# Depthwise convolution of the latent steps as products with diagonal matrices, with bias and SiLU at the bank's reading

## The reference, cut to what matters

```python
def depthwise_conv_centred(u, w, b):          # u (1, N, 768), w (768, 5), b (768,)
    ch, width = w.shape
    rhs = jnp.transpose(w)[:, None, :].astype(u.dtype)
    out = lax.conv_general_dilated(u, rhs, window_strides=(1,), padding=[(width // 2, width // 2)],
                                   dimension_numbers=("NWC", "WIO", "NWC"), feature_group_count=ch)
    return out + b

xbc = jax.nn.silu(depthwise_conv_centred(xbc, lp["ssd_conv_w"], lp["ssd_conv_b"]))
```

## Time and profile before

| what | value |
|---|---|
| median of 3 runs | 2536.7 us (2534.78 to 2538.18) |
| the profiled execution's own time | 2540.28 us |
| its span, first to last instruction | 2538.4 us |
| PE busy | 1435.2 us (57%) |
| DVE busy | 1544.1 us (61%) |
| ACT busy | 272.6 us (11%) |
| POOL busy | 1460.7 us (58%) |
| DMA | 969.43 MB, mean 382 GB/s |
| mean granted PE clock | 0.715 of full |

### The profile page before, as it was taken

One profiled execution on the slowest core, in us unless ns is written; L12 is line 12 of the kernel. 1 busy time (PEld: TensorE's weight loads), 2 busy tenths in 40 slices (PEclk: granted clock), 3 DMA queues, 4 the chain that ended last, 5 costly groups with the idle time before them and its releaser, 6 DMA issues.

```text
span 2538.4 us, 20653 instructions
## 1 busy us (share of the span) xinstructions
PE 1435.2 (57%) x6676; PEld 610.3 (24%) x6676; DVE 1544.1 (61%) x4131; ACT 272.6 (11%) x667; POOL 1460.7 (58%) x1540
## 2 busy tenths in 40 slices
PE   6899757897332544365557786888510333332365
PEld 2455522372011211013212253356000000000000
DVE  0348975687887456556472687487799545457501
ACT  1321131111000010010000122211000000000000
POOL 0003527546657567766666646554747777777772
PEclk9889877997666656667767787799655555665666
DMA  9987999999979999999999999998969999999997
GB/s 371 403 336 294 395 380 382 370 404 374 378 288 411 413 410 410 410 411 412 412 411 377 379 412 342 373 351 337 395 253 406 409 409 409 409 409 410 410 409 301
DMA packets 238045, 969.43 MB, mean 382 GB/s; under 512 B 26314, under 2 KB 28746, under 8 KB 227954
## 3 DMA queue, kind: packets, MB, share of 16 engines
q0 software_dynamic: 221184, 805.40, 80.6%
q1 hardware_dynamic: 16754, 162.71, 15.6%
HBM read 964.87 MB, written 3.15 MB: 381 GB/s over the span
## 4 chain that ended last, share of the span: by engine, by line
DMA 37%; PE 22%; DVE 18%; POOL 14%; issue 7%; ACT 2%; SPq 0%; DVEq 0%; ACTq 0%; POOLq 0%
DMA ring<-peer_v_in,vidx 17%; POOL ring L645 8%; DMA work<-peer_v_in,vidx 7%; DMA work<-peer_u_in,idx 7%; DVE ring L1798 6%; PE psum L978 6%; POOL work L645 5%; DMA ring<-peer_u_in,idx 4%; PE acc L1024 4%; PE psum L954 3%; DVE work L1798 2%; PE psum L735 2%; POOL wring L645 2%; PE psum L690 1%; PE acc L662 1%
## 5 line engine op out<-in xcount | busy, mean ns | idle before, releaser
L645 POOL DMA_INDIRECT ring<-peer_u_in,idx x492 | 465.0, 945 | 523.5 <-DVE idx L1491 207.8
L1798 DVE CUSTOM_DVE_ANT_0 ring<-ring,h_kept 128x1024 f32<-128x1024 f32 x492 | 581.8, 1218 | 256.8 <-DMA ring<-peer_u_in,idx 249.4
L645 POOL DMA_INDIRECT ring<-peer_v_in,vidx x478 | 459.7, 962 | 252.8 <-issue 119.4
L1024 PE MATMUL acc<-ring,vw 128*32 128x512 f32 x1752 | 341.0, 852 | 365.7 <-DMA ring<-peer_v_in,vidx 340.0
L1798 DVE CUSTOM_DVE_ANT_0 work<-work,h_kept 128x1024 f32<-128x1024 f32 x208 | 249.8, 1220 | 178.7 <-DMA work<-peer_u_in,idx 173.0
L1024 PE MATMUL acc<-work,vw 128*32 128x512 f32 x672 | 150.3, 931 | 324.7 <-DMA work<-peer_v_in,vidx 306.3
L645 POOL DMA_INDIRECT work<-peer_v_in,vidx x226 | 215.0, 951 | 100.9 <-issue 57.2
L645 POOL DMA_INDIRECT work<-peer_u_in,idx x208 | 196.7, 946 | 117.8 <-issue 54.0
L1024 PEld LDWEIGHTS acc<-ring,vw 128*32 128x32 f32 x1752 | 49.9, 128 | 609.4 <-issue 595.4
L735 PE MATMUL psum<-wring,work 128*128 128x512 f32 (+1 forms) x432 | 176.2, 566 | 18.7 <-ACT work L1097 11.5
L978 PE MATMUL psum<-work,wring 128*128 128x256 f32 (+1 forms) x896 | 167.4, 352 | 2.9 <-ACT work L1066 2.9
(11 more groups left out here) (226 smaller groups left out, 1696.0 us busy)
## 6 DMA issues: line engine op xcount, KB each, us to landing
wring<-w_in_in SPq DMA_DIRECT2D x17, 2048.0 KB, 10.4
wring<-peer_wq_in SPq DMA_DIRECT2D x14, 2048.0 KB, 10.4
wring<-mod_w_in SPq DMA_DIRECT2D x10, 2048.0 KB, 13.1
ring<-mod_w_in SPq DMA_DIRECT2D x9, 2048.0 KB, 10.7
wring<-w_out_in SPq DMA_DIRECT2D x8, 2048.0 KB, 10.6
work<-mod_w_in SPq DMA_DIRECT2D x5, 2048.0 KB, 14.2
ring<-peer_u_in,idx POOLq DMA_INDIRECT x492, 11.9
ring<-peer_v_in,vidx POOLq DMA_INDIRECT x478, 8.5
```

Of the source, the lines that this page charges most:

```text
L645: nc.gpsimd.indirect_dma_start(slots[slot_of[n]], None, table, bass.IndirectOffsetOnAxis(ap=at[:, col + r:col + r + 1], axis=0))\
L1024: ins = mm(acc[half][lane:lane + QUAD, :], w[:, at:at + QUAD], two[j - pair][0][:, half * CHUNK:(half + 1) * CHUNK], start=(r == 0), stop= ...
L1798: V.tensor_tensor_reduce(held, held, h_kept[:, :], 1.0, 0.0, ALU.mult, ALU.add, dots[:, dots_at(k, t) + r:dots_at(k, t) + r + 1]).then_inc ...
```

## The change

In the latent steps (`st.lat`) the middle taps on ACT and the 24 tap additions on DVE go. For each block ACT makes five 128x128 diagonal matrices, each the identity scaled by the per-partition tap weight; two sets of five are held in `L.diag`, in the space of the rotary scratch, so the first two wait for the rotary embedding to be done, and each later set waits for the product that used its space. PE makes per block five products of a diagonal with `xraw` shifted by the tap into one bank, and ACT reads the bank with SiLU and the bias. The context steps keep their way. The first two sets of diagonals stand on ACT ahead of "conv", that is ahead of the pooling carries; the products stand on PE after the pooling mixer and, in k = 1, after its modulation chunks.

```diff
+            L.diag = [region(14104 + i * TAPS * P, TAPS * P) for i in range(2)]
...
-                pe.wait_ge(*after("conv", k))
+                if st.lat:
+                    pe.wait_ge(*after("padded", k))
+                    for b in range(CONV_BLOCKS):
+                        p = job(pe, "cv", k, b)
+                        pe.wait_ge(*taken("xb", k, b))
+                        pe.wait_ge(*after("diag", k, b))
+                        for j in range(TAPS):
+                            ins = mm(p[:, 0:N], st.L.diag[b % 2][:, j * P:(j + 1) * P], st.L.xraw[:, b, j:j + N],
+                                     start=(j == 0), stop=(j == TAPS - 1))
+                        ins.then_inc(*made("cv", k, b))
+                    pe.wait_ge(*taken("cv", k, CONV_BLOCKS - 1))
+                else:
+                    pe.wait_ge(*after("conv", k))
...
+            def diagonals(st, b):
+                if b >= 2:
+                    act.wait_ge(*full("cv", st.k, b - 2))
+                for j in range(TAPS):
+                    ins = A(st.L.diag[b % 2][:, j * P:(j + 1) * P], ident, ACT.Copy, scale=conv_w[:, b, j:j + 1])
+                ins.then_inc(*mark("diag", st.k, b))
...
                 for b in (4, 5):
-                    middle_tap(st, b)
+                    if not st.lat:
+                        middle_tap(st, b)
                     carry(st.L.xraw[:, b, 2:2 + N], bank("xb", k, b)[:, 0:N], "xb", k, b)
...
+                if st.lat:
+                    act.wait_ge(*after("rope", k, T - 1))
+                    diagonals(st, 0)
+                    diagonals(st, 1)
                 yield "conv"
...
-                act.wait_ge(*after("conv_sum", k))
-                A(st.L.conv[:, :, 0:N], st.L.conv[:, :, 0:N], ACT.Silu).then_inc(*mark("conv", k))
+                if st.lat:
+                    for b in range(CONV_BLOCKS):
+                        act.wait_ge(*full("cv", k, b))
+                        A(st.L.conv[:, b, 0:N], bank("cv", k, b)[:, 0:N], ACT.Silu, bias=conv_b[:, b:b + 1])\
+                            .then_inc(*take("cv", k, b))
+                        if b + 2 < CONV_BLOCKS:
+                            diagonals(st, b + 2)
+                else:
+                    act.wait_ge(*after("conv_sum", k))
+                    A(st.L.conv[:, :, 0:N], st.L.conv[:, :, 0:N], ACT.Silu).then_inc(*mark("conv", k))
...
-                d(V.memset(st.L.xraw[:, :, N + 2:N + 4], 0.0))
+                V.memset(st.L.xraw[:, :, N + 2:N + 4], 0.0).then_inc(*mark("padded", k))
...
-                for b in range(CONV_BLOCKS):
-
-                    dve.wait_ge(*taken("xb", k, b))
-                settle()
-                for j in OTHER_TAPS:
+                if not st.lat:
...
```

More of the change, by code:

```diff
@@ L158 @@
 par_lam lam mx aw o_n h2 x_mid topk_diff topk_exp picked act_done gelu vw acc_free x_new y_ready
-pool_step act_step v_step sums o_done h_kept""".split()
+padded diag pool_step act_step v_step sums o_done h_kept""".split()
 def build_pass(nc, io, where, known):
@@ L1603, in dense @@
                                 a_log.unsqueeze(1).broadcast_to([P, T, 8]), ALU.mult).then_inc(*mark("dta", k))
-                for b in range(CONV_BLOCKS):
-                    dve.wait_ge(*taken("xb", k, b))
-                settle()
-                for j in OTHER_TAPS:
+                if not st.lat:
                     for b in range(CONV_BLOCKS):
[L1611 to L1616, removed]
-                    settle()
+                        dve.wait_ge(*taken("xb", k, b))
+                    dve.wait_ge(*after("padded", k))
+                    settle()
+                    for j in OTHER_TAPS:
+                        for b in range(CONV_BLOCKS):
+                            o, src, w = st.L.conv[:, b, 0:N], st.L.xraw[:, b, j:j + N], conv_w[:, b, j:j + 1]
+                            ins = V.scalar_tensor_tensor(o, src, w, o, ALU.mult, ALU.add)
+                            if j == OTHER_TAPS[-1] and b == CONV_BLOCKS - 1:
+                                ins.then_inc(*mark("conv_sum", k))
+                            else:
+                                d(ins)
+                        settle()
                 yield "dt"
```

## The result

| | kernel before | changed kernel |
|---|---|---|
| median | 2537.44 us (8 runs, 2534.21 to 2543.73) | 2550.93 us (8 runs, 2545.92 to 2556.15) |
| ratio, 95% interval | | 1.0053 [1.0038, 1.0068] |
| span of the profiled execution | 2538.4 us | 2551.4 us |
| DVE busy | 1544.1 us | 1525.7 us |
| PE busy | 1435.2 us | 1465.6 us |

The changed kernel is slower, by 13.5 us between the medians. DVE was relieved of 18.4 busy us, and the time did not follow it.

A forecast was written before the change was run, and what follows sets the result against it. The prediction took DMA row gathers to bound the kernel, time being lost where DVE's ring slots come late. 2540.28 + 5.3 + 5.6 = 2551.2 us, 2547.5 against the median; forecast's own range 2541 to 2555, overall 2534 to 2562.

The forecast's parts named there:

- What bounds: Whole kernel: row gathers fill the DMA; time is lost where it runs dry, set by DVE's order of freeing ring slots.
- the rule of the Trainium skill that I set against the forecast: Whole kernel: improvement comes from the busiest engine first, so neither DVE's relief nor PE's load would show.
- The products: PE, each latent step: thirty products at 0.432 us each, 13.0 us at full clock, 26 us at half.
- ACT: ACT in the convolution loop: 2.0 us a turn, covered by PE's 2.16 us; first ten diagonals 2.9 us.
- First step: First latent step, to segments and decay mixing: +5.3 us, between +4 and +8, the wait for the third chunk hiding the rest.
- Second step: Second latent step: pooling waits for the band table, 7.4 us to land; `xw` at 1526.7, +5.6 us.
- Sum: Whole kernel: 2540.28 + 5.3 + 5.6 = 2551.2 us for the profiled execution, 2547.5 us against the median.
- A (the DMA takes it up): Whole kernel: the busiest DMA repays the delay where it now runs dry; same time, 2533 to 2542 us; chance 0.15.
- B (DVE's time counts): Latent steps: tap additions lie on the chain in full; one step gains 10 us, 2527 us; chance 0.13.
- C (cold PE): Latent steps: PE's clock stays low, products take 26 us; 2560 us for one step, 2573 for both; chance 0.10.
- Signs: Changed profile: products about 13 us, `xw` near 358 and 1527, first segments near 362, DMA dip about 1527.
- POOL's wait in the first step: POOL, first latent step: its wait for a slot from DVE would be longer than 13.91 us.

The follow-up runs named there:

- no taps: Kernel before with the 24 tap additions of both latent steps left out, nothing put in their place; 0.9979 and, repeated, 0.9992 of the kernel before.
- one product: Changed kernel with the middle tap alone, one diagonal and one product a block instead of five; 0.9987 of the kernel before.
- moved: Changed kernel with the same products placed in PE's idle time, diagonals behind the carries; 0.9988 and, repeated, 0.9993 of the kernel before.
- first step only: Kernel before with the change in the first latent step alone, run twice on slower chips; 1.0009 and 1.0004 of the kernel before.
- The second profile: Profile from running the unaltered changed kernel again beside the kernel before; 1.0063 of it, medians 2550.19 against 2536.69 us.
- the second step alone: Kernel before with the change in the second latent step alone; 1.0021 of the kernel before, +4.4 us by the medians.

## Why the prediction was right

*What bounds.* Right. DVE's relief is worth nothing that can be measured (no taps), and the products cost by the length of their stage (one product). Where they stand decides (moved). That the cost is passed on by the ring slots, and not by the dense work behind the stretch, is argued and not shown. By the rule of the Trainium skill that I set against the forecast ("Perfetto Trace Analysis", section "Identifying the Most-Contended Engine") there would have been no change; the measured one is outside 0.2%. The Trainium skill itself speaks of kernels in which the most contended engine changes over time (same page, section "Optimization Strategy"), and that fits here: in these 50 us the row sets under way run out (DMA share 0.35 at 360 to 365), and the chain PE, ACT, DVE decides.

*The products.* 13.0 us forecast, 13.61 measured in both steps. The price of 0.432 us held in the shorter turns of the loop, 2.16 us for five; over the whole stage there is 0.1 us a block on top. The Trainium skill's 109 ns for 256 columns ("TensorE: Matmul & The Clock Gate", section "Back-to-back issue gap") is not what a float32 product costs here.

*ACT.* 2.0 us a turn forecast, 2.16 - 0.23 = 1.93 measured; ten diagonals 2.9 us forecast, 3.02 measured. PE paced the loop.

*First step.* +5.3 forecast, +7.0 measured. The step that failed is "PE ends its modulation chunks at 342.6 as before": they ended at 346.2. Half of these 3.6 us is the whole step, which begins 1.8 us later in this execution; counted from the zeroing of the padding, the chunks end 1.9 us later. With the 0.6 us that products and last SiLU took more than forecast this makes 2.5 us, of which 0.8 came back behind them. What delayed the chunks is in the rows. PE waited 1.23 us for the pooling carries behind the diagonals, whose 2.9 us I had charged to ACT alone; this wait is in the first step of every profile that has the ten diagonals there, 1.2 to 1.3 us in the changed kernel and 2.3 us in the first step only. The cumulative sums took 1.0 us and the pooling products 0.8 us more, at half clock. In return PE no longer waited 0.82 us for the second chunk, and the first had landed 0.4 us earlier in the step. The windows of before and after show the clock:

```profile
330.00:335.00 5.00, 3.85 (x34) 3.40 (x32) 4.62 (x13) 1.04 (x3) 3.40 (x4) 0.96 0.96 395
...
330.00:335.00 5.00, 5.00 (x25) 3.57 (x18) 0.46 (x4) 0.24 (x1) 0.00 (x0) 0.50 0.99 410
```

The later rise of the clock isn't tied to the change. The sixteen records of the q/k transposes took 3.65 us in both profiles of the changed kernel, but also 3.65 and 3.27 us in the two of no taps, which has neither products nor diagonals, and 1.94 us in both of the first step only, which has the changed kernel's first step. Why it rises early or late stays open. The third chunk on a running PE gave 1.7 us back, as forecast.

*Second step.* +5.6 forecast for `xw` and the mixing. Measured from the zeroing, `xw` came 7.5 us later (37.7 against 30.2) and the mixing 6.6 us. The wait in place of DVE's is the band table, as forecast. The term that was too small is its landing: 9.23 us and not 7.4. With an issue 0.2 us later, pooling starts 2.1 us later than forecast. The 7.4 is the median of two loads of the table; the one of this step took 6.4 us in the kernel before. Behind `xw`, DVE gave 0.9 us back, since it no longer waited between the two scalings (0.43 us) and less for the chunk states (0.22 and not 0.77 us). The second profile had a stretch 8.3 us longer, but 1.7 us of that is DVE's earlier start: from the cumulative sums both profiles are 6.3 and 6.4 us longer than before.

*Sum.* 10.9 us forecast, 13.5 measured, 2547.5 against 2550.93 us. The two terms missed 1.7 and 1.0 us. That their sum as measured in one profile, 13.6 us, agrees with the difference of the medians to 0.1 us is luck: executions of one kernel differ by several us behind the second stretch.

*Rivals.* A (the DMA takes it up): the whole change leaves it out; that a part is taken up in the second step alone (4.4 of 5.4 us by the medians) is within the error. B (DVE's time counts): fell with the no-taps kernel; `xw` of the second step came later than before and not earlier. C (cold PE): the products ran at full clock both times; it was the work ahead of them in the first step that was cold.

*Signs.* The products, `xw`, the segments and the dip of the DMA came within some 2 us of their places once the later start of each step is taken off (1.8 and 8.7 us). POOL's wait in the first step was longer than 13.91 us, but at another place than I had in mind: the 24.37 us stand behind `xw`, while the wait behind the decay mixing, the 13.91 of before, is now 4.36 us.

## What to carry to other kernels

An engine's relief is worth what its wait's successor leaves of it: before moving work, ask which wait ends next in that stretch, here the load of a weight chunk in one step and of the band table in the other, and the gain ends there. The moved work costs what no wait of the receiving engine covers: of 27.2 us of products in two steps, half was covered where they stood. So it belongs ahead of a wait that the receiving engine has anyway; the same sixty products cost 13.5 us at one place and nothing that could be measured at another. And a stretch measured from an instruction of one engine to one of another holds how far the two were apart at its start; measure from the engine whose work was changed as well. Products with a diagonal are a dear way to scale channels in float32: five products of 0.432 us took the place of four additions on DVE, 0.415 us each in their row of 24, and a reading of the bank on ACT.

## What the runs showed of the hardware that I had not expected

The same program takes 2537 us on one chip and 2760 and 2766 us on two others, with the compute instructions of the same length: thirty products took 13.60 us and a dot product 1.22 us on either kind. The DMA moved a mean of 380 to 384 GB/s on the first kind and 349 to 352 on the second. The slower chips also blur differences more: the intervals reach 5 to 8 us to either side there and 3 to 5 us on the faster one, so a difference of 5 us can't be told on them even from a dozen runs beside some thirty of the kernel before.

The clock of PE rose at different times behind almost the same wait. The changed kernel and the first step only have one PE program up to the first pooling mixer of k = 1. Behind a wait of 14.14 us the sixteen transpose records took 1.94 us in the latter, behind one of 14.18 us they took 3.65 us in the former (on different chips). So a difference of some 2 us in such a stretch says nothing of the edit before several profiles agree.
